# Cached K turned in place on VectorE, its scores as 32 by 32 products in four row bands and four banks, and a ring of 24 pages

## What is computed

```python
x <- LN(alpha*x + 1/2*(1+g1)*SwiGLU_1(x*(1+s1)+b1))
x <- LN(alpha*x + (1+g2)*W_o[MoBA heads | GLA heads](x*(1+s2)+b2))
x <- LN(alpha*x + 1/2*(1+g3)*SwiGLU_2(x*(1+s3)+b3))
```

```python
k_past = cache_k[layer, page_table].reshape(B, past, H, HD)
kmean = mean over each block of 256 rows of k_past       # 8 blocks
idx = top_k(q . kmean, 3)                                # per query row
s_sel = q . k of the chosen blocks * HD**-0.5
s_own = q . k_new * HD**-0.5, causal
p = softmax(concatenate([s_sel, s_own]))
o = p_sel @ v_sel + p_own @ v_new
```

## Time and profile before

| | |
|---|---|
| median of the runs | 982.14 us |
| the profiled execution's own time | 983.45 us |
| its span | 981.3 us |
| mean granted clock | 0.961 of full |
| PE, DVE, ACT busy over the span | 94%, 56%, 37% |
| HBM read | 195.00 MB |
| mixer's input projections end, first transposes of cached K begin | 446.7 us |
| first product of the output projection | 670.0 us |

### The profile page before, as it was taken

One profiled execution on the slowest core, in us unless ns is written; L12 is line 12 of the kernel. 1 busy time (PEld: TensorE's weight loads), 2 busy tenths in 40 slices (PEclk: granted clock), 3 DMA queues, 4 the chain that ended last, 5 costly groups with the idle time before them and its releaser, 6 DMA issues.

```text
span 981.3 us, 17319 instructions
## 1 busy us (share of the span) xinstructions
PE 919.1 (94%) x6991; PEld 798.8 (81%) x6991; DVE 545.9 (56%) x839; ACT 359.5 (37%) x509; POOL 28.1 (3%) x34
## 2 busy tenths in 40 slices
PE   6999999999999899999878999859899999989997
PEld 2588888988999599996665877548779999989994
DVE  0545444454655677785843538443666765554655
ACT  1424322232442534454642426240333232323433
POOL 0000000000000000000000000001200000000000
PEclk9999999998999999999999889877999999999999
DMA  9899889886456744448858998996416465534511
GB/s 329 258 299 258 240 244 257 245 235 169 127 152 191 256 129 145 144 153 268 297 190 325 324 325 310 356 343 199 125 39 167 133 163 139 145 89 122 155 50 53
DMA packets 214885, 199.93 MB, mean 204 GB/s; under 512 B 9569, under 2 KB 161261, under 8 KB 214678
## 3 DMA queue, kind: packets, MB, share of 16 engines
q1 hardware_dynamic: 213412, 194.99, 64.8%
q0 software_dynamic: 704, 2.49, 0.7%
q10 hardware_dynamic: 690, 1.35, 0.4%
HBM read 195.00 MB, written 3.80 MB: 203 GB/s over the span
## 4 chain that ended last, share of the span: by engine, by line
PE 83%; DVE 6%; ACT 3%; SPq 3%; issue 2%; DMA 2%; ACTq 0%; DVEq 0%
PE B L691 20%; PE B L692 19%; PE B L696 19%; PE B L751 4%; PE B L887 3%; PE B L898 2%; SPq L619 2%; PE B L936 2%; PE B L775 2%; PE B L760 2%; PE B L791 2%; DMA ring<-in_cache_v 1%; PE B L1017 1%; PE B L717 1%; PE B L712 1%
## 5 line engine op out<-in xcount | busy, mean ns | idle before, releaser
L691 PE MATMUL B<-Hh,wh 128*128 128x320 f32 x912 | 274.2, 314 | 0.6 <-issue 0.6
L692 PE MATMUL B<-Hl,wh 128*128 128x320 f32 x912 | 270.5, 310 | 0.0
L1595 DVE TENSOR_TENSOR wl<-raw,wh 128x2048 fp32r<-128x2048 f32 x90 | 207.3, 2305 | 94.3 <-ACT wh L1240 94.0
L1240 ACT ACTIVATE wh<-raw 128x2048 fp32r<-128x2048 f32 x90 | 172.3, 1914 | 150.3 <-PE B L696 117.6
L691 PEld LDWEIGHTS B<-Hh,wh 128*128 128x128 f32 x912 | 172.4, 189 | 10.7 <-issue 10.0
L692 PEld LDWEIGHTS B<-Hl,wh 128*128 128x128 f32 x912 | 172.4, 189 | 0.3
L696 PE MATMUL B<-Hh,wl 128*128 128x320 f32 x912 | 152.8, 310 | 0.0
L696 PEld LDWEIGHTS B<-Hh,wl 128*128 128x128 f32 x912 | 139.1, 189 | 0.0
L691 PE MATMUL B<-Gh,wh 128*128 128x320 f32 x352 | 107.1, 317 | 2.5 <-DVE Gl L1721 2.5
L692 PE MATMUL B<-Gl,wh 128*128 128x320 f32 x352 | 106.7, 316 | 0.0
L1240 ACT ACTIVATE sg<-B 128x320 f32<-128x320 f32 x46 | 20.1, 438 | 210.1 <-PE B L696 195.7
(11 more groups left out here) (246 smaller groups left out, 951.8 us busy)
## 6 DMA issues: line engine op xcount, KB each, us to landing
raw<-in_w_ffn_in SPq DMA_DIRECT2D x88, 512.0 KB, 6.2
raw<-in_w_ada SPq DMA_DIRECT2D x72, 512.0 KB, 4.9
ring<-in_cache_k SPq DMA_DIRECT2D x108, 256.0 KB, 5.3
ring<-in_cache_v SPq DMA_DIRECT2D x84, 256.0 KB, 5.0
raw<-in_w_ffn_out SPq DMA_DIRECT2D x32, 384.0 KB, 3.6
raw<-in_w_mix_in SPq DMA_DIRECT2D x24, 512.0 KB, 4.7
raw<-in_w_ffn_out SPq DMA_DIRECT2D x32, 320.0 KB, 4.3
M<-in_cache_v SPq DMA_DIRECT2D x16, 256.0 KB, 4.5
```

Of the source, the lines that this page charges most:

```text
L691: pe.matmul(out, w, xh[k], start=start and k == 0, stop=False)
L692: pe.matmul(out, w, xl[k], start=False, stop=False)
L1240: return act.activation(out, in_, func, **kw)
L1595: dve.tensor_tensor(wl[:, wbuf(n), :], raw_view(n), f32(wh[:, wbuf(n), :]), ALU.subtract).then_inc(lo_ready, 1)
```

## The change

1. K is no longer transposed on TensorE. VectorE transposes a landed group in place, as blocks of 32 by 32 over 128 x 2048 (turn_keys, now VectorE's, one instruction for each group). After that partition 32a + r of a page holds, at 32m + j, row 32a + j, column 32m + r of the page as it was. The tile kT and its 128 copies are gone.
2. The scores of 8 pages of one sample (a chunk) are 64 products with a contraction of 32 rows: row band a (which 32 rows of the page), column band c (which pair of heads), and x (which 32 of the pair's 128 columns), summed over x and over the two samples. Row band a has its own PSUM bank: the tile S4 covers banks 0 to 3. The queries have to lie four times, once for each row band (Qs, made from Qz by turn_queries on TensorE and queries_out on ScalarE, once for each sample).
3. There is one set of score banks for both halves s = 0, 1 of a pair. ScalarE copies it to prob in four instructions of 128 x 256 that also sum the block (the gate), and VectorE takes the maximum from prob (block_max) where it took sum and maximum from PSUM.
4. K pages are used when the scores of their chunk are done, where they were used when they had been transposed.
5. The ring has 24 pages (6 buffers), the two new ones in the place of wh, the halved weights. M now gives three buffers for the last pair and W one. K goes to pairs of buffers, V to the one that was free first. IN_H ends earlier. The last two ring buffers end with pair 2.
6. The points of mix move: k = 0 to 6 at points 0 to 6, 12 to 19 at 7 to 14, four points for each pair. Three banks turn where five did. probs_act takes one bank more from VectorE. MO's first two tiles land in W.
7. Qz lies in a dead part of the constants and is set to zero later on GpSimd.

```diff
-GROUPS = RING // 4
+GROUPS = 6
-AT_POINT = {0: 0, 1: 1, 3: 2, 4: 3, 5: 4, 6: 5, 8: 6, 9: 12, 10: 13, 11: 14, 13: 15, 14: 16, 15: 17, 16: 18, 18: 19}
+AT_POINT = {x: x if x <= 6 else x + 5 for x in range(15)}
...
+USE = [key for s in range(2) for bi in range(2) for key in key_groups(0, s, bi)]
...
+        USE += key_groups(_i + 1, 0, 0) + key_groups(_i + 1, 0, 1) + value_groups(_i, 0)
+        USE += key_groups(_i + 1, 1, 0) + value_groups(_i, 1) + key_groups(_i + 1, 1, 1)
...
+PAGE_GROUPS = [key for key in USE if key != ("v", 0, 0, 0)]
+PAGE_GROUPS.insert(6, ("v", 0, 0, 0))
...
+LAST_IN = {IN_H: GROUP_AT[("v", 1, 3, 1)], 4: GROUP_AT[("k", 3, 3, 1)], 5: GROUP_AT[("k", 3, 3, 1)]}
...
-                    sp.wait_ge(tp_filled, FILL_AT[("k", i, g, bi, 3)] + 1)
+                    sp.wait_ge(s_out, chunk(i, g // 2, bi) + 1)
...
+            def turn_queries(i, bi):
+                bank = turn_bank(("q", i, bi))
+                if i == 0:
+                    pe.wait_ge(q_ready, 4)
+                for x in range(4):
+                    for q in range(4):
+                        m = pe.matmul(bank[32 * q:32 * q + 32, P * x:P * (x + 1)], ident[:, 32 * x:32 * x + 32],
+                                      Qz[:, 2 * i + bi, :, :].rearrange("p c r -> p (c r)"), start=True, stop=True)
+                m.then_inc(tp_filled, 1)
+            def scores(i, s, bi):
+                if bi == 0 and 2 * i + s >= 1:
+                    pe.wait_ge(s_act, 2 * i + s)
+                if s == 0:
+                    wait_act(("q", i, bi))
+                pe.wait_ge(k_turned, 2 * chunk(i, s, bi) + 2)
+                b = BUF[GROUP_AT[("k", i, 2 * s, bi)]]
+                for x in range(4):
+                    for a in range(4):
+                        for c in range(HP):
+                            f = P * c + 32 * x
+                            m = pe.matmul(S4[32 * c:32 * c + 32, a, 0:256].rearrange("r (p j) -> r p j", p=8),
+                                          Qs[32 * a:32 * a + 32, bi, x, c, :],
+                                          ring[32 * a:32 * a + 32, 4 * b:4 * b + 8, f:f + 32],
+                                          start=(bi == 0 and x == 0), stop=(bi == 1 and x == 3))
+                m.then_inc(s_out, 1)
...
             for i in range(NPAIR):
+                m0 = 4 * i + 3
                 if i + 1 < NPAIR:
-                    turn_keys(i + 1, 0, 0)
-                    turn_keys(i + 1, 0, 1)
                     point(m0)
-                    scores(i + 1, 0)
-                    turn_keys(i + 1, 1, 0)
-                    turn_keys(i + 1, 1, 1)
+                    scores(i + 1, 0, 0)
                     point(m0 + 1)
-                    scores(i + 1, 1)
+                    scores(i + 1, 0, 1)
+                    point(m0 + 2)
                     turn_probs(i)
-                    point(m0 + 2)
                     values(i, 0)
-                    turn_keys(i + 1, 2, 0)
-                    turn_keys(i + 1, 2, 1)
                     point(m0 + 3)
+                    scores(i + 1, 1, 0)
+                    if i + 2 < NPAIR:
+                        turn_queries(i + 2, 0)
                     values(i, 1)
-                    scores(i + 1, 2)
                     own_scores(i + 1)
-                    turn_keys(i + 1, 3, 0)
-                    turn_keys(i + 1, 3, 1)
-                    point(m0 + 4)
-                    scores(i + 1, 3)
+                    scores(i + 1, 1, 1)
...
+            def scores_out(i, s):
+                act.wait_ge(s_out, chunk(i, s, 1) + 1)
+                if i >= 1:
+                    wait_fill(("p", i - 1, 4))
+                for m in range(4):
+                    n = 4 * s + m
+                    last = act_(prob[:, BLK * n:BLK * (n + 1)].rearrange("p (q a j) -> p a q j", q=2, a=4),
+                                S4[:, :, 64 * m:64 * m + 64].rearrange("p a (q j) -> p a q j", q=2),
+                                accum_out=gate[:, n:n + 1])
+                last.then_inc(s_act, 1)
...
+            def turn_keys(i, s, bi):
+                for g in (2 * s, 2 * s + 1):
+                    n = GROUP_AT[("k", i, g, bi)]
+                    b = BUF[n]
+                    dve.wait_ge(page_landed[b], 64 * TURN_IN[n])
+                    v = ring[:, 4 * b:4 * b + 4, :].rearrange("p j f -> p (j f)")
+                    dve.transpose(out=v, in_=v).then_inc(k_turned, 1)
+            def block_max(i, s):
+                dve.wait_ge(s_act, 2 * i + s + 1)
+                dve.tensor_reduce(bmax[:, 4 * s:4 * s + 4],
+                                  prob[:, 4 * BLK * s:4 * BLK * (s + 1)].rearrange("p (n k) -> p n k", n=4), X_AXIS,
+                                  ALU.max).then_inc(dve_step, 1)
...
             for i in range(NPAIR):
+                m0 = 4 * i + 3
+                block_max(i, 1)
+                choose(i)
                 if i >= 1:
                     out_low(i - 1)
                 if i + 1 < NPAIR:
+                    turn_keys(i + 1, 0, 0)
                     point(m0)
+                    turn_keys(i + 1, 0, 1)
                     point(m0 + 1)
+                    point(m0 + 2)
+                    totals(i)
                     probs_dve(i, 1)
+                    probs_dve(i, 4)
+                    point(m0 + 3)
+                    block_max(i + 1, 0)
+                    turn_keys(i + 1, 1, 0)
+                    own_heads(i)
+                    own(i + 1)
+                    turn_keys(i + 1, 1, 1)
```

More of the change, by code:

```diff
@@ L135, in mix_fills, with key_groups, value_groups, chunk @@
     return fills
-def key_fills(i, j):
-    return [("k", i, j, bi, p) for bi in range(2) for p in range(4)]
-PAGE_GROUPS = [("k", 0, j, bi) for j in range(4) for bi in range(2)]
+def key_groups(i, s, bi):
+    return [("k", i, 2 * s, bi), ("k", i, 2 * s + 1, bi)]
+def value_groups(i, bi):
+    return [("v", i, g, bi) for g in range(4)]
+def chunk(i, s, bi):
+    return 4 * i + 2 * s + bi
 GAPS = [[] for _ in range(12)]
@@ L151 @@
     GAPS[6 + _lv] += mix_fills(7 + _lv)
+GAPS[7] += [("q", 0, bi) for bi in range(2)]
 GAPS[8] += [("nv", t) for t in range(3)]
@@ L184 @@
+        USE += key_groups(_i + 1, 1, 0) + value_groups(_i, 1) + key_groups(_i + 1, 1, 1)
+        FILLS += [("q", _i + 2, 0)] if _i + 2 < NPAIR else []
+        FILLS += [("own", _i + 1)]
+        FILLS += [("q", _i + 2, 1)] if _i + 2 < NPAIR else []
+    else:
+        USE += value_groups(_i, 0) + value_groups(_i, 1)
+    FILLS += [("pick", _i)]
+PAGE_GROUPS = [key for key in USE if key != ("v", 0, 0, 0)]
+PAGE_GROUPS.insert(6, ("v", 0, 0, 0))
 GROUP_AT = {key: n for n, key in enumerate(PAGE_GROUPS)}
+USE_AT = {key: n for n, key in enumerate(USE)}
@@ L191, in place_groups @@
+LAST_IN = {IN_H: GROUP_AT[("v", 1, 3, 1)], 4: GROUP_AT[("k", 3, 3, 1)], 5: GROUP_AT[("k", 3, 3, 1)]}
 def place_groups():
[L193 to L199, removed]
+    free = {(MI + x) % R: x - 30 for x in range(8, 12)} | {4: -9, 5: -8, IN_H: -7}
+    at, last, buf, before = {}, {}, [], []
+    for n, key in enumerate(PAGE_GROUPS):
+        for b in FIRST_IN:
+            if n == FIRST_IN[b]:
+                free[b] = -1
+        kind, i, g, bi = key
+        if kind == "k" and g % 2 == 0:
+            d = min(range(GROUPS // 2), key=lambda d: (max(free[2 * d], free[2 * d + 1]), d))
+            at[key], at["k", i, g + 1, bi] = 2 * d, 2 * d + 1
+            free[2 * d] = free[2 * d + 1] = USE_AT["k", i, g + 1, bi]
+        elif kind == "v":
+            b = min([b for b in free if n <= LAST_IN.get(b, n)], key=lambda b: (free[b], -b))
+            at[key], free[b] = b, USE_AT[key]
+        b = at[key]
@@ L266, in shape_constants @@
     parts["cos"], parts["sin"] = cos, sin
+    reset = np.ones((P, N))
+    reset[:, [0] + [S + T * b for b in range(NB)]] = 0.0
+    parts["reset"] = reset
     q = p[:, None]
@@ L378, in layer_kernel @@
             small = sb("small", [P, 192], F32, mixer)
[L380 to L381 removed]
+        with ExitStack() as low_banks:
+            B = [low_banks.enter_context(nc.psum_tensor(f"B{i}", [P, 512], F32)) for i in range(4)]
+        S4 = ctx.enter_context(nc.psum_tensor("S4", [P, 4, 512], F32))
+        B += [ctx.enter_context(nc.psum_tensor(f"B{i}", [P, 512], F32)) for i in range(4, 8)]
+        OB = 4
         def split_view(t, n, kind):
@@ L933, in values @@
                         pe.wait_ge(om_ready, i)
+                    elif g == 0 and bi == 0:
+                        last = [n for n in range(IN_MI) if BANK[n] == OB][-1]
+                        pe.wait_ge(*((tp_act, act_through(last)) if on_act(FILLS[last]) else (tp_dve, dve_through(last))))
                     for p in range(4):
```

271 lines of the change are left out of this document (84 added, 187 removed).

## The result

The change makes the kernel slower: 1020.01 us, the median of four runs (1014.45 to 1020.93), against 981.44 (978.08 to 983.33) in the same session. The ratio is 1.0385 with a 95% interval of [1.0338, 1.0432]. The forecast was 976, so it missed by 44 us, and on the wrong side.

A forecast was written before the change was run, and what follows sets the result against it. No engine full, nearest TensorE (85%) and DMA (80%), with DMA underfed for 44 us of the stage. Later choose(3), 5.4, less 12 in the tail gave -6.6: 977 us against 983.45; point 976, range 957 to 1003.

The forecast's parts named there:

- The chain of a pair: Serial work from one choose to the next: cycles of 53, 58.5 and 54 us, 165.5 for 160.4 before.
- cycle 3: Last choose-to-choose cycle, from the maximum of pair 2 to that of pair 3: 54 us where the row has 47.8.
- Scores on TensorE: Score products of a chunk, 128 instructions at 27 ns: 3.5 us a chunk, 56 us for 16 chunks.
- Rival C: Score products on TensorE: row bands do not run beside one another, 54 ns each; +27, about 1003 us; chance 0.11.
- Transposes on VectorE: 32 added transposes of 128 x 2048 on VectorE: 2.25 us each, 4.5 a chunk, 72 us.
- rival D: VectorE's transpose takes twice the row, 4.5 us more a chunk; +43, about 1020 us; chance 0.07.
- Balance of VectorE and ScalarE: Work in the stage: VectorE 18 us more, 135 of some 220; ScalarE falls by 26 us.
- The start: Projections and first chunk's turning, before the first scores: +2 us, bounds 0 to 5.
- The tail: Last pair, choose to last values: no V-buffer waits within the pair, 15.5 us instead of 27.5, 12 less.
- Rival E: TensorE's clock falls, a pair's mean from 0.92 to 0.8: +10, about 985 us; chance 0.11.
- Rival A: Products are quick and the loads decide: 13 to 20 us more gain, some 960 us; chance 0.20.
- What would show it: Signs in the stage's trace; against: scores over 35 ns, transposes over 3 us, K-score waits idling DMA over 40 us.

The follow-up runs named there:

- e5_turns_first: The changed kernel with VectorE's transposes of chunks (i+1,1,0), (i+1,0,0) and (i+1,1,1) moved ahead of what stood before them; 979.55 us, ratio to before 1.0004.
- e10_first_small: e5_turns_first with each VectorE transpose cut from 128 x 2048 to 128 x 32, nearly all of K left unturned; 967.33 us, one run.
- e7_less_v: e5_turns_first with only 128 of 512 columns of V loaded for groups in later turns of ring buffers; 978.07 us, one run.

## Why the prediction was wrong

**The step that failed** is "The chain of a pair". It let chunk (i+1,1,0) be turned as soon as its pages had landed ("7.5; turn 4.5, scores 3.5"). The one point of mix in its sum, "a point of mix (3)", is the one between the first two transposes of a cycle. The point and the maximum that stand ahead of turn_keys(i+1,1,0) in VectorE's program have no term in it, and that point waits for TensorE, whose products stand behind values(i,0). The diff shows both programs; the prediction never laid them beside each other. In cycle 3 the sum puts the turned chunk's scores to their end 33.3 us after choose (2.3 + 4.5 + 3 + 4.5 + 3.5, then 7.5 + 4.5 + 3.5), at 652.6 us; they end at 666.8, and the 14 us between are more than the whole miss of that cycle (12.5). The Trainium skill ("Perfetto Trace Analysis", Tensor Engine Instruction) states that ACT, DVE and GPSIMD are strict FIFO; the timeline above agrees, with 6.96 us of an idle VectorE and landed pages behind a waiting instruction. In the kernel before, the turning stood in TensorE's own program and VectorE only copied a part of it to kT; TensorE's matmuls waited 1.8 us in all for those copies in the stage.

By the forecast's own terms (choose(0) at 480, cycles 53, 58.5 and 54, tail 15.5, from first scores at 449):

| | forecast | the change | e5_turns_first |
|---|---|---|---|
| first scores to choose(0) | 31 | 30.7 | 30.9 |
| cycle 1 | 53 | 64.1 | 55.1 |
| cycle 2 | 58.5 | 75.7 | 59.0 |
| cycle 3 | 54 | 66.5 | 54.5 |
| tail, to the end of the values | 15.5 | 20.3 | 20.1 |

The values of the forecast end at 661 us and those of the change at 706. Of these 45 us the three cycles account for 40.8 and the tail for 4.8, less 0.5 ahead of choose(0). With the order mended the cycles come out within 2.1, 0.5 and 0.5 us. That closeness is partly luck. Errors inside the cycles cancel: chunks at the lower clock are longer, and all transposes together cost 11.2 us over the three cycles by e10_first_small, not 13.5 us each. And e5_turns_first turns (i+1,0,0) ahead of choose, where the forecast's sum has it behind. The kernel with only the waits that the sum left out taken away was not run.

- *Scores on TensorE*: right, and quicker. A chunk of 128 instructions goes in 2.75 us at a granted clock of 1.00 (448.83 us), 21 ns each, where 27 was taken (3.5 us). At a granted clock of 0.50 (536.14 us) it takes 4.5. Rival C (row bands one after another, 54 ns) is false. The Trainium skill ("TensorEngine Tiling (Array Packing)", Instruction Overhead) would have made it 25 ns; the measured step is shorter.
- *Transposes on VectorE*: right, 2.25 us apart (4.50 for two) and 72 us in all; rival D is false.
- *Balance of VectorE and ScalarE*: 135 us forecast for VectorE, 132.5 measured; 67 for ScalarE (93 - 26), 67.7 measured.
- *The start*: +2 forecast, first scores at 449. Measured 448.83. The agreement says little, since the first scores of the variants lie between 443.88 and 449.18 us with the same projections ahead of them; the term is within that scatter and is not shown.
- *The tail*: no wait behind a V buffer any more, as forecast, and 7 us shorter than before. But 4.8 longer than forecast, 4.1 of it in the values: 11.7 us from the first to the end of the last, not 7.6. TensorE runs at the lower level there (0.52 granted from 694.26 to 699.23):

```profile
694.26 1.93 PE L971 MATMUL B<-W,PT 128*32 128x128 f32 x32
695.97 3.43 PE L971 MATMUL B<-M,PT 128*32 128x128 f32 x64
...
704.70 1.08 PE L971 MATMUL B<-ring,PT 128*32 128x128 f32 x32 [1.25 <-DMA ring<-in_cache_v]
```

  The first 96 instructions take 5.0 us (694.26 to 699.23), 52 ns each, against the 27 ns of the earlier trace rows; the last 32 wait 1.25 us for their page.
- *Rival E*: the clock did fall, to 0.75 in the stage and not to 0.8, and the price of 10 us for it cannot be told in the changed kernel apart from the order; in e5_turns_first the fillers raised the clock and won nothing, but their own work stands against it, so the price stays open.
- *Rival A*: the quick products came and the gain did not; in e7_less_v a quarter less of the stage's loads won nothing.
- *What would show it*: the prediction named more than 40 us of idle DMA in the stage, with SyncE waiting for K's scores, as a sign against it. That is what came: 79.4 us of such waits, and 83 us idle by the estimate above. (By the same estimate the kernel before had 44 us idle, so the waits are the sign and not the 40.)

The gain that was expected, with the order mended, is 0 and not 6: the time from the first scores to choose(0) wins 2.1 us (30.9 for 33.0) and the tail 7.4, and the cycles take back 8.2 (168.6 for 160.4 us). The forecast's cycles took back 5.1, and its tail won 12.

## What to carry to other kernels

When work moves to another engine, its place in that engine's program is part of its price: write the in-order programs of both engines side by side, and for each moved instruction name what stands ahead of it, and what that waits for. If that is a product of the engine which in turn waits for the moved work, the two take turns where they should overlap, and every link of the ring looks like the culprit when it is shortened. Mend the order first, and test the suspected costs then: here fillers worth 14 us of the stage on the changed kernel, and transposes worth 31, were worth next to nothing and 12 afterwards.

## What the runs showed of the hardware

- Sixteen tiles of 32 rows by 32 columns of TensorE (four row bands by four column bands, each row band with its own PSUM bank) run beside one another: an instruction with 256 moving columns each 21 ns at a granted clock of 1.00 (2.75 us for 128) and 35 ns at 0.50 (4.52 us). Four column bands alone take 27 ns for 128 columns.
- A VectorE transpose of 128 x 2048 float32 in blocks of 32 by 32, in place, takes 2.25 us, the time of an elementwise operation of that size (2.29 us in the earlier trace rows).
- TensorE stops in the middle of a chunk of scores without anything in the trace that it waits for ("issue"), 6.1 us in four waits in the changed kernel's stage and 8.2 us in six in e5_turns_first, the longest 3.5 us:

```profile
502.76 2.56 PE L928 MATMUL S<-ring,Qs 32*32 32x256 f32 x106 [1.09 <-DVE ring L1792]
508.82 1.13 PE L928 MATMUL S<-ring,Qs 32*32 32x256 f32 x22 [3.50 <-issue]
```

  (e5_turns_first.) What holds it up there was not tried.
